# Chunked state-space scan in a decoder trunk: exponentials of the decay sums stored once and loaded per chunk, gate SiLUs in three batches, half products on another schedule

## The chip, the core and the metric

The program runs on one core of one Trainium2 chip. A core has a matrix engine (PE, with weight loads shown apart as PEld), a vector engine (DVE), a scalar engine for activation functions (ACT), a general engine (POOL) and a queue engine (SP) that mainly issues DMAs. Each has its own in-order stream of instructions, and the streams meet only at semaphores. The metric is the device time of one execution in microseconds (us); lower is better.

## What is computed

A trunk of two pre-norm residual layers on 1024 tokens of width 1024. Layer 0 mixes with windowed attention and pooling, layer 1 with a Mamba-2 style scan (SSD); each is followed by a dense SwiGLU. The change is in the scan of layer 1, in this part of the reference:

```python
def ssd_chunked(x, dt, A, Bm, Cm):          # L = 128 tokens, 8 chunks, G = 4 groups of 8 heads
    dA = (dt * A).reshape(b, nc, L, G, hg)
    a_cs = jnp.moveaxis(jnp.cumsum(dA, axis=2), 2, -1)          # the decay sums
    seg = a_cs[..., :, None] - a_cs[..., None, :]
    decay = jnp.exp(jnp.where(causal, seg, -jnp.inf))
    cb = jnp.einsum('bclgn,bcsgn->bcgls', Cc, Bc)
    y_diag = jnp.einsum('bcgls,bcghls,bcsghp->bclghp', cb, decay, xdt)
    ...
    y_off = jnp.einsum('bclgn,bcghpn,bcghl->bclghp', Cc, prev, jnp.exp(a_cs))
    return (y_diag + y_off).reshape(b, s, h, p)
```

Afterwards `y = (scan + x*D) * silu(z)`, where z is one more projection of the input, then a grouped RMS norm and the output projection.

## The kernel before

The matrix products run as three products of split operands (`mm3`: high by high, low by high, high by low, lines L1377 to L1379), so that PE has three 512-column matmuls for each block of 128 inputs. ACT makes the high halves (`hi`, a Copy, L892) and POOL the low ones (`lo`, a subtraction, L721).

The scan stage (`ssd_group`, one function on each engine) runs four times, once for each group of 8 heads: three trips of a loop and a copy behind it. One group is:

- Six projections of 1024 tokens (B, C and four blocks of x) with a short convolution: ACT starts `acc` (L1273), DVE adds three shifted taps (L2448), ACT takes the SiLU (L1282).
- Eight chunks c = 0 to 7 of 128 tokens. For each chunk the row of decay sums comes from DRAM, broadcast over the partitions into `mdec[c % 2]` (L664, a DMA on SP's queue, which for c of 2 and more waits until PE's product of chunk c - 2 has used the buffer). ACT takes `exp` of it into `eacs[c % 2]`, as two activations of 64 partitions (L1301), and then turns `mdec` into the decays in place: eight Relu with a bias per head (L1308) and two Exp over four heads each (L1313). DVE multiplies each half by the masked product of C and B (L2487, `m_ready`). PE has, in this order: the transposes and the C by B product of chunk c + 1 (L1808 to L1813), the states (L1832), the contribution of the carried state (L1837, "yoff"), the diagonal product (L1845, 16 small matmuls, "ydiag"), which waits for both halves of `mdec` and for DVE's `yx` of chunk c - 1, and then some half products of the gate. DVE adds up: token-major copies of chunk c + 1 (`cbm` L2461, `btok` L2464, `xdt` L2468), the state (L2499), `eacs` times yoff (L2506), plus ydiag (L2509), and four `yx` (L2516, `y_ready`). POOL scales `xds` (L846) and `decayed` (L849), and makes the low halves of weights where `LO_AFTER_CHUNK` says.
- The gate z: eight units n (four blocks, two token halves), each made of the half products 2n and 2n + 1, 12 matmuls of 512 columns each. `Z_AFTER_CHUNK` says behind which chunk's ydiag PE does which half products; halves 2 and 3 stand in the code ahead of chunk 0.
- The end: DVE multiplies by the gate (L2476), ACT squares and makes `y_hi` (L1323, L1324), DVE `y_lo` (L2526), and PE starts the output projection (the L1377 rows with `y_hi`), which waits for the `y_lo` of a block before it uses the block. Three outputs are begun with three blocks each before the fourth block is asked for.

The sums themselves are made once ahead of the four groups; DVE copies their transpose to `sumT` and ACT's queue stores it to DRAM (L1257).

Of the kernel before, what the change touches and what calls it, by code (L numbers as in the profile page):

```python
# [27 lines left out]
F32 = mybir.dt.float32  # L28
F32R = mybir.dt.float32r
ALU = mybir.AluOpType  # L30
ACT = mybir.ActivationFunctionType
# [61 lines left out]
def trunk(nc, x, mix_norm_w, ap_w_in, ap_sinks, pool_w, pool_scale, ap_w_out, ssd_w_in, ssd_conv_w,  # L93
# [40 lines left out]
    with ExitStack() as ctx:  # L134
# [79 lines left out]
        gda_lo = at("gda_lo", 4 * S + G * NT * HG, [G * NT * HG], F32R)  # L214
        sumT = at("sumT", 4 * S + 2 * G * NT * HG, [2, P])
        ones = at("ones", 10240 + 3 * NK * SH, [P], F32R)

# [74 lines left out]
        hidden = nc.dram_tensor("hidden", (NP, P, 7 * BANK), F32, kind="Internal").ap()  # L292
        decay_sums = nc.dram_tensor("decay_sums", (G, NT, HG * P), F32, kind="Internal").ap()

        def tail_pair(tt):
# [28 lines left out]
        def down_banks(layer, j):  # L324
# [9 lines left out]
        LO_AFTER_CHUNK = {1: (9,), 2: (10,), 6: (11,), 7: (12, 13)}  # L334
        Z_AFTER_CHUNK = {-1: (0, 1), 0: (4,), 1: (5, 6), 2: (7,), 3: (8, 9), 4: (10, 11), 5: (12,), 6: (13,),
                         7: (14, 15)}
        SILU_AFTER_CHUNK = {1: (0, 1), 3: (2, 3), 5: (4, 5), 7: (6,)}
        GATE_AFTER_CHUNK = {6: (0, 1)}
# [160 lines left out]
        cb_freed, xdt_ready, m_ready = sem("cb_freed"), sem("xdt_ready"), sem("m_ready")  # L499
        relu_done, dec_ready, e_ready = sem("relu_done"), sem("dec_ready"), sem("e_ready")  # L500
        xds_ready, decayed_ready = sem("xds_ready"), sem("decayed_ready")
# [22 lines left out]
        def _(sp):  # L524
# [130 lines left out]
            def ssd_group(g):  # L655
                piece = in_group(g)
                firsts = [g + bc_, g + cc_] + [g * BG + xc + b for b in range(BG)] + [g * BG + zc + b for b in range(BG)]

                def load_decay(c):

                    if c >= 2:
                        sp.wait_ge(ydiag_full, t.count("chunk", c - 1))
                    src = decay_sums[g:g + 1, c, :] if isinstance(g, int) else decay_sums[bass.ds(g, 1), c, :]
                    sp.dma_start(mdec[c % 2][:, :, :].rearrange("p h l -> p (h l)"), src.to_broadcast([P, HG * P]))\  # L664
                        .then_inc(decay_loaded[c % 2], 16)

                for k in range(GP):
                    if k < NCB + BG:
                        load(piece(k), blocks[:, :, bass.ds(firsts[k], 1), :].rearrange("p k j c -> p k (j c)"))
                    else:  # L670
                        b = k - NCB - BG
                        load(piece(k), rows[:, bass.ds(g * BG + b, 1), :].rearrange("p j n -> p (j n)"))
                    if k == 7:
                        sp.wait_ge(sums_stored, 16)
                        load_decay(0)
                    if k == 8:
                        sp.wait_ge(silu_done, t.count("silu", NCB - 1))
                        load_decay(1)
                    for c in DECAY_AFTER_PIECE.get(k, ()):
                        load_decay(c)  # L680
                t.add("chunk", NT)
                t.add("silu", NCB)
# [194 lines left out]
        def _(act):  # L877
# [366 lines left out]
            for k in range(2, LEAD):  # L1244
# [11 lines left out]
            act.wait_ge(sumT_ready, 1)  # L1256
            act.dma_start(decay_sums.rearrange("g c (h l) -> (g c h) l", l=P).rearrange("(a r) l -> r a l", r=P), sumT[:, :, :])\  # L1257
                .then_inc(sums_stored, 16)
            act.wait_ge(dts_v, 5)
            for d, first in ((D[3], GC_DS), (D[7], GC_CD)):  # L1260
                act.activation(gconst[:, :, first:first + NT * HG],
                               d[:, :, :].rearrange("p c s -> p (c s)").rearrange("p (g k) -> p g k", g=G), ACT.Exp)\
                    .then_inc(dts_a, 1)
            t.add("unit")

            def ssd_group(g, last=False):
# [25 lines left out]
                for c in range(NT):  # L1293
                    m = mdec[c % 2]
                    act.wait_ge(decay_loaded[c % 2], t.count("loaded", 16 * (c // 2 + 1)))

                    if c >= 2:
                        act.wait_ge(y_ready, t.count("chunk", c - 1))
                    for odd in range(2):
                        rows = slice(64 * odd, 64 * odd + 64)  # L1300
                        ins = act.activation(eacs[c % 2][rows, :, :], m[rows, odd::2, :], ACT.Exp)  # L1301
                    ins.then_inc(e_ready, 1)
                    act.wait_ge(e_ready, t.count("chunk", c + 1))

# [600 lines left out]
        def _(dve):  # L1906
            t = Tally(unit=0, out=0, tile=0, conv=0, z=0, chunk=0, half=0, carry=0, group=0, rms=0, tail=0,
                      step=0, xhi=0)

# [527 lines left out]
            def ssd_group(g, last=False):  # L2437
# [41 lines left out]
                for c in range(NT):  # L2479
# [20 lines left out]
                    else:  # L2500
                        dve.tensor_copy(state[:, :], ps[:, STATES, :]).then_inc(state_ready, 1)
                    dve.wait_ge(e_ready, t.count("chunk", c + 1))
                    e = eacs[c % 2]
# [15 lines left out]
                t.add("half", 2 * NT)  # L2519
                t.add("carry", NT - 1)  # L2520

                def lo(b, h):
# [46 lines left out]

            dve_loop = dict(unit=NCB, conv=NCB, z=2 * BG, chunk=NT, half=2 * NT, out=2 * NT, carry=NT - 1, group=1, rms=2)  # L2570
            with dve.Fori(0, G - 1) as g:
# [27 lines left out]
```

## Time and profile before

| what | us |
|---|---|
| median of 3 runs | 2396.69 |
| lowest and highest | 2395.57, 2397.83 |
| the profiled execution, own time | 2397.36 |
| its span, first to last instruction | 2395.6 |
| PE busy in it | 2310.4 (96%) |
| POOL, DVE and ACT busy | 1210.8, 1281.2 and 1072.4 |

The span and what lies around it (1.8 us) make the execution's own time. Busy times of different engines overlap. A timeline row gives the start, the duration, the engine and line, the operation, how many instructions are merged in the row, and in brackets how long the engine had been idle before it and what ended that. Durations of neighbours on one engine overlap a little, so a step from start to start is what an instruction costs in a row. A matmul of 512 columns takes 0.23 us from start to start in the stretches where PE's granted clock is 1.0.

### The profile page before, as it was taken

To read this page: it belongs to the slowest core of one execution; us is meant where nothing else is said; L and a number is where in the kernel's file an instruction comes from. 1 tells how busy PE (TensorE), PEld (TensorE's weight loads), DVE (VectorE), ACT (ScalarE), POOL (GpSimd) and SP (SyncE) were. 2 spreads that over 40 slices of the span, in tenths; PEclk is the share of its full clock that TensorE was granted. 3 is DMA by queue.
4 is the path that set the end of the run, shared out by engine and by line. 5 is a ranking of instruction groups with operands and counts; after the bars stand their busy time and mean duration, and the time that the engine had idled before them with its cause. 6 is when DMAs were issued, how large, how long until landed. Compare 5 with 4: busy or idle time off the path is not lost.

```text
span 2395.6 us, 29381 instructions
## 1 busy us (share of the span) xinstructions
PE 2310.4 (96%) x10850; PEld 1880.6 (79%) x10850; DVE 1281.2 (53%) x1660; ACT 1072.4 (45%) x1887; POOL 1210.8 (51%) x852
## 2 busy tenths in 40 slices
PE   6998999999999999999999999999999999999997
PEld 5876778888887788687887887887778888888786
DVE  5446573324334787557348338437772333335776
ACT  4035553333333445457248238239553333333444
POOL 3123278777773554224214314223288778774553
PEclk9999999999999999999999999999999999999999
DMA  5100213223227743221212112122213223227744
GB/s 154 46 27 18 87 63 121 102 108 114 84 97 257 245 150 111 73 63 62 64 43 88 45 53 92 32 71 80 89 62 132 107 91 114 84 97 273 246 149 144
DMA packets 166786, 247.89 MB, mean 103 GB/s; under 512 B 18416, under 2 KB 111484, under 8 KB 164092
## 3 DMA queue, kind: packets, MB, share of 16 engines
q1 hardware_dynamic: 161020, 230.06, 29.1%
q10 hardware_dynamic: 5632, 15.99, 1.7%
q8 instruction: 90, 1.47, 0.3%
q14 instruction: 44, 0.36, 0.0%
HBM read 192.93 MB, written 53.08 MB: 103 GB/s over the span
## 4 chain that ended last, share of the span: by engine, by line
PE 82%; DVE 7%; POOL 3%; ACT 3%; issue 3%; DMA 1%; SPq 0%; DVEq 0%; ACTq 0%; POOLq 0%
PE ps L1377 26%; PE ps L1379 25%; PE ps L1378 25%; POOL p_lo L746 1%; PE ps L1845 1%; POOL p_val L770 1%; DVE acc L2448 1%; PE ps L1400 1%; PE ps L1832 1%; DVE mdec L2487 1%; DMA d_val<-in_w_down 1%; DVE yx L2516 1%; PE ps L1837 1%; PE ps L1563 1%; PE ps L1542 0%
## 5 line engine op out<-in xcount | busy, mean ns | idle before, releaser
L721 POOL TENSOR_TENSOR w_lo<-w_raw,w_hi 128x1024 fp32r<-128x1024 f32 x74 | 182.4, 2468 | 361.0 <-ACT w_hi L892 361.0
L823 POOL TENSOR_TENSOR s_lo<-s_val,s_hi 128x512 fp32r<-128x512 f32 x154 | 231.6, 1507 | 220.4 <-ACT s_hi L1188 220.2
L2119 DVE TENSOR_TENSOR xres<-ps,xres 128x512 f32<-128x512 f32 x132 | 90.7, 688 | 436.6 <-PE ps L1379 425.5
L1377 PE MATMUL ps<-xn_hi,w_hi 128*128 128x512 f32 x800 | 317.9, 397 | 5.6 <-DVE acc L2448 2.6
L1378 PE MATMUL ps<-xn_lo,w_hi 128*128 128x512 f32 x800 | 312.8, 391 | 0.0
L1379 PE MATMUL ps<-xn_hi,w_lo 128*128 128x512 f32 x800 | 312.6, 391 | 0.0
L1377 PE MATMUL ps<-xn_hi,p_hi 128*128 128x512 f32 x704 | 276.3, 392 | 8.9 <-POOL p_lo L746 4.6
L1378 PE MATMUL ps<-xn_lo,p_hi 128*128 128x512 f32 x704 | 275.2, 391 | 0.0
L1379 PE MATMUL ps<-xn_hi,p_lo 128*128 128x512 f32 x704 | 275.1, 391 | 0.0
L746 POOL TENSOR_TENSOR p_lo<-p_val,p_hi 128x512 fp32r<-128x512 f32 x176 | 238.8, 1366 | 43.8 <-ACT p_hi L1007 43.8
L1007 ACT ACTIVATE p_hi<-p_val 128x512 fp32r<-128x512 f32 x176 | 111.1, 632 | 313.4 <-POOL p_val L770 312.4
L1377 PE MATMUL ps<-d_hi,s_hi 128*128 128x512 f32 x616 | 241.5, 392 | 7.4 <-DVE xres L2183 3.4
L1378 PE MATMUL ps<-d_lo,s_hi 128*128 128x512 f32 x616 | 240.4, 390 | 0.0
L1379 PE MATMUL ps<-d_hi,s_lo 128*128 128x512 f32 x616 | 240.2, 390 | 0.0
L1377 PEld LDWEIGHTS ps<-xn_hi,w_hi 128*128 128x128 f32 x800 | 150.8, 189 | 43.1 <-issue 9.8
L2448 DVE SCALAR_TENSOR_TENSOR acc<-ps,gc,acc 128x1023 f32<-128x1023 f32 (+2 forms) x72 | 92.3, 1281 | 172.3 <-ACT acc L1273 170.6
L1188 ACT ACTIVATE s_hi<-s_val 128x512 fp32r<-128x512 f32 x154 | 97.0, 630 | 177.5 <-DMA d_val<-in_w_down 100.7
L1379 PEld LDWEIGHTS ps<-xn_hi,w_lo 128*128 128x128 f32 x800 | 150.9, 189 | 32.1
L1378 PEld LDWEIGHTS ps<-xn_lo,w_hi 128*128 128x128 f32 x800 | 151.1, 189 | 30.1
L892 ACT ACTIVATE w_hi<-w_raw 128x1024 fp32r<-128x1024 f32 x74 | 77.4, 1052 | 208.0 <-PE ps L1379 181.8
L1377 PEld LDWEIGHTS ps<-xn_hi,p_hi 128*128 128x128 f32 x704 | 132.9, 189 | 38.3 <-POOL p_lo L746 6.0
L1379 PEld LDWEIGHTS ps<-xn_hi,p_lo 128*128 128x128 f32 x704 | 133.0, 189 | 27.7
(271 smaller groups left out, 5074.9 us busy)
## 6 DMA issues: line engine op xcount, KB each, us to landing
s_val<-hidden SPq DMA_DIRECT2D x154, 256.0 KB, 2.8
hidden<-xres SPq DMA_DIRECT2D x20, 1792.0 KB, 6.4
wv_g<-in_w_gate SPq DMA_DIRECT2D x22, 1024.0 KB, 5.1
wv_u<-in_w_up SPq DMA_DIRECT2D x22, 1024.0 KB, 5.1
w_raw<-in_ssd_w_in SPq DMA_DIRECT2D x40, 512.0 KB, 3.8
d_val<-in_w_down SPq DMA_DIRECT2D x70, 256.0 KB, 3.8
rows_v<-in_w_down SPq DMA_DIRECT2D x64, 256.0 KB, 3.5
mdec<-decay_sums SPq DMA_DIRECT2D x32, 512.0 KB, 3.7
```

Of the source, the lines that this page charges most:

```text
L721: pool.tensor_tensor(w_lo[piece.slot][:, :], raw[piece.raw][:, :], f(w_hi[piece.slot][:, :]), ALU.subtract).then_inc(lo_done, 1)
L746: pool.tensor_tensor(p_lo[n][:, :, :], src, f(p_hi[n][:, :, :]), ALU.subtract).then_inc(p_lo_done, 1)
L770: pool.tensor_tensor(p_val[n][:, :, :], a, b, op).then_inc(sum_ready, 1)
L823: pool.tensor_tensor(s_lo[i][:, :], s_val[i][:, :], f(s_hi[i][:, :]), ALU.subtract)\
L892: act.activation(w_hi[piece.slot][:, :], raw[piece.raw][:, :], ACT.Copy).then_inc(hi_done, 1)
L1007: act.activation(p_hi[n][:, :, :], src, ACT.Copy).then_inc(p_hi_done, 1)
L1188: act.activation(s_hi[i][:, :], s_val[i][:, :], ACT.Copy).then_inc(s_hi_done, 1)
L1377: pe.matmul(dst, l_hi, r_hi, start=first, stop=False, skip_group_check=reopened)
L1378: pe.matmul(dst, l_hi, r_lo, start=False, stop=False, skip_group_check=reopened)
L1379: return pe.matmul(dst, l_lo, r_hi, start=False, stop=last, skip_group_check=reopened)
L2119: dve.tensor_tensor(tmp, bank, tmp, ALU.add).then_inc(c_ready, 1)
L2448: ins = dve.scalar_tensor_tensor(acc[k % 2][:, shift:], full[:, 0:S - shift], gc[:, tap:tap + 1], acc[k % 2][:, shift:], ALU.mult, ALU.add)
```

## The change

`exp` of the decay sums is taken once, on the transposed sums (`sumE`), ahead of the groups, and stored by ACT's queue to a second DRAM tensor. Per chunk two more DMAs on SP's queue bring it into `eacs`, broadcast over 64 partitions each (`load_e`), behind the load of `mdec` of the same chunk. For c of 2 and more `load_e` waits for `y_ready` of chunk c - 2. ACT loses the two Exp activations per chunk and its wait for `y_ready`; DVE waits for the loads instead of for ACT. The first load of decays waits for both stores. The two tables `Z_AFTER_CHUNK` and `SILU_AFTER_CHUNK` change.

```diff
-        Z_AFTER_CHUNK = {-1: (0, 1), 0: (4,), 1: (5, 6), 2: (7,), 3: (8, 9), 4: (10, 11), 5: (12,), 6: (13,),
-                         7: (14, 15)}
-        SILU_AFTER_CHUNK = {1: (0, 1), 3: (2, 3), 5: (4, 5), 7: (6,)}
+        Z_AFTER_CHUNK = {-1: (0, 1), 0: (4, 5), 1: (6,), 2: (7, 8), 3: (9,), 4: (10, 11), 5: (12,), 6: (13, 14),
+                         7: (15,)}
+        SILU_AFTER_CHUNK = {1: (0, 1, 2), 4: (3, 4, 5), 7: (6,)}
...
+                def load_e(c):
+
+                    if c >= 2:
+                        sp.wait_ge(y_ready, t.count("chunk", c - 1))
+                    src = decay_exps[g:g + 1, c, :] if isinstance(g, int) else decay_exps[bass.ds(g, 1), c, :]
+                    src = src.rearrange("a (b o l) -> a o b l", o=2, l=P)
+                    for odd in range(2):
+                        sp.dma_start(eacs[c % 2][64 * odd:64 * odd + 64, :, :],
+                                     src[:, odd].to_broadcast([64, BG, P])).then_inc(e_loaded[c % 2], 16)
...
-                        sp.wait_ge(sums_stored, 16)
+                        sp.wait_ge(sums_stored, 32)
                         load_decay(0)
                     if k == 8:
                         sp.wait_ge(silu_done, t.count("silu", NCB - 1))
                         load_decay(1)
+                        load_e(0)
+                        load_e(1)
                     for c in DECAY_AFTER_PIECE.get(k, ()):
                         load_decay(c)
+                        load_e(c)
...
+            act.activation(sumE[:, :, :], sumT[:, :, :], ACT.Exp).then_inc(sumE_ready, 1)
+            act.wait_ge(sumE_ready, 1)
+            act.dma_start(sums_of(decay_exps), sumE[:, :, :]).then_inc(sums_stored, 16)
...
-                    if c >= 2:
-                        act.wait_ge(y_ready, t.count("chunk", c - 1))
-                    for odd in range(2):
-                        rows = slice(64 * odd, 64 * odd + 64)
-                        ins = act.activation(eacs[c % 2][rows, :, :], m[rows, odd::2, :], ACT.Exp)
-                    ins.then_inc(e_ready, 1)
-                    act.wait_ge(e_ready, t.count("chunk", c + 1))
...
-                    dve.wait_ge(e_ready, t.count("chunk", c + 1))
+                    dve.wait_ge(e_loaded[c % 2], t.count("loaded", 32 * (c // 2 + 1)))
```

ACT's stream before, from the SiLUs behind chunk 3 to the decays of chunk 6 (chunk 4 and 6 use the first `mdec`, chunk 5 the second; `zs` and `ps` at L1290 are the SiLUs of units 2, 3 and then 4, 5):

```order
L1290 ACTIVATE zs_115<-ps 128x512
L1290 ACTIVATE zs_116<-ps 128x512
L1301 ACT_TABLE_LOAD
L1301 ACTIVATE eacs_100<-mdec_92 64x512 x2
L1308 ACTIVATE mdec_92<-mdec_92,gc 128x128 x8
L1313 ACTIVATE mdec_92<-mdec_92 128x512 x2
L1301 ACTIVATE eacs_101<-mdec_93 64x512 x2
L1308 ACTIVATE mdec_93<-mdec_93,gc 128x128 x8
L1313 ACTIVATE mdec_93<-mdec_93 128x512 x2
L1290 ACT_TABLE_LOAD
L1290 ACTIVATE ps<-ps 128x512 x2
```

The same stretch of the changed kernel, from the decays of chunk 4 (first `mdec`) to those of chunk 5 (second). The SiLUs of units 3, 4 and 5 are at L1310, the Relu at L1319, the Exp at L1324:

```order
L1319 ACTIVATE mdec_93<-mdec_93,gc 128x128 x8
L1324 ACTIVATE mdec_93<-mdec_93 128x512 x2
L1310 ACT_TABLE_LOAD
L1310 ACTIVATE zs_117<-ps 128x512
L1310 ACTIVATE ps<-ps 128x512 x2
L1319 ACTIVATE mdec_94<-mdec_94,gc 128x128 x8
L1324 ACT_TABLE_LOAD
L1324 ACTIVATE mdec_94<-mdec_94 128x512 x2
```

What moved: the SiLU of unit 5 stood behind the decays of chunk 5, and stands ahead of them now. The half products that it waits for, 10 and 11, are behind ydiag of chunk 4 in both kernels.

SP's queue in the changed kernel, last group, from the loads for chunk 2 on (`w_raw` is a piece of the output weights):

```order
L667 DMA mdec_93<-decay_sums 128x1024 [waits ydiag_full]
L677 DMA eacs_101<-decay_exps 64x4x128 [waits y_ready]
L677 DMA eacs_101<-decay_exps 64x4x128
L667 DMA mdec_94<-decay_sums 128x1024 [waits ydiag_full]
L677 DMA eacs_102<-decay_exps 64x4x128 [waits y_ready]
L677 DMA eacs_102<-decay_exps 64x4x128
L543 DMA w_raw<-in_ssd_w_out 128x1024 [waits lo_done] x2
```

What moved: before, the two `mdec` loads and the two weight loads followed each other; now each `mdec` load is followed by two loads of `eacs`, the first of which can hold up what stands behind it.

## Rows read from the trace of the kernel before

**Rows 1.** The page's busy times and its chain, shares of the span by engine.
```profile
PE 2310.4 (96%) x10850; PEld 1880.6 (79%) x10850; DVE 1281.2 (53%) x1660; ACT 1072.4 (45%) x1887; POOL 1210.8 (51%) x852
PE 82%; DVE 7%; POOL 3%; ACT 3%; issue 3%; DMA 1%; SPq 0%; DVEq 0%; ACTq 0%; POOLq 0%
```
**Rows 2.** Waits of PE over the span: total us, times, longest.
```profile
PE ps L1845 <- DVE mdec L2487: 14.5, 13, 2.6
...
PE ps L1377 <- DVE acc L2448: 2.6, 1, 2.6
```
**Rows 3.** PE's timeline, second group: chunks 1, 5, 6, 7.
```profile
1255.92 1.09 PE L1845 MATMUL ps<-mdec,xdt 128*64 128x128 f32 x16 [0.79 <-DVE mdec L2487]
...
1287.43 0.38 PE L1808 MATMUL ps<-CT,BT 128*128 128x128 f32 x2
...
1290.05 1.09 PE L1845 MATMUL ps<-mdec,xdt 128*64 128x128 f32 x16
...
1296.83 1.09 PE L1845 MATMUL ps<-mdec,xdt 128*64 128x128 f32 x16 [0.23 <-DVE mdec L2487]
...
1305.19 1.09 PE L1845 MATMUL ps<-mdec,xdt 128*64 128x128 f32 x16 [2.53 <-DVE mdec L2487]
1306.22 0.50 PE L1377 MATMUL ps<-xn_hi,w_hi 128*128 128x512 f32 x1
...
1311.79 0.39 PE L1377 MATMUL ps<-w_hi,y_hi 128*128 128x512 f32 x1
```
**Rows 4.** ACT's timeline, second group, from chunk 5's decays to chunk 6's.
```profile
1280.51 1.15 ACT L1313 ACTIVATE mdec<-mdec 128x512 f32<-128x512 f32 x2
...
1287.63 0.58 ACT L1290 ACTIVATE ps<-ps 128x512 f32<-128x512 f32 x1 [4.08 <-PE ps L1379]
1288.13 1.05 ACT L892 ACTIVATE w_hi<-w_raw 128x1024 fp32r<-128x1024 f32 x1
1289.19 1.28 ACT L1301 ACT_TABLE_LOAD   x1
1290.49 1.27 ACT L1301 ACTIVATE eacs<-mdec 64x512 f32<-64x512 f32 x2
1291.79 2.45 ACT L1308 ACTIVATE mdec<-mdec,gc 128x128 f32<-128x128 f32 x8
1294.27 1.15 ACT L1313 ACTIVATE mdec<-mdec 128x512 f32<-128x512 f32 x2
```
**Rows 5.** DVE's timeline, second group: chunks 0 and 2, then chunk 6 on.
```profile
1250.70 3.96 DVE L2516 SCALAR_TENSOR_TENSOR yx<-yx,gc,eacs 128x128 f32<-128x128 f32 x4
...
1265.93 0.68 DVE L2506 TENSOR_TENSOR eacs<-ps,eacs 128x512 f32<-128x512 f32 x1
...
1297.70 1.27 DVE L2476 TENSOR_TENSOR yx<-ps,yx 128x512 f32<-128x512 f32 x2
...
1303.86 1.28 DVE L2487 TENSOR_TENSOR mdec<-mdec,cbm 128x512 f32<-128x512 f32 x2
...
1307.13 1.19 DVE L2516 SCALAR_TENSOR_TENSOR yx<-yx,gc,eacs 128x128 f32<-128x128 f32 x4
...
1308.85 3.55 DVE L2526 SCALAR_TENSOR_TENSOR y_lo<-yx,gc,y_hi 128x512 fp32r<-128x512 f32 x3
```
**Rows 6.** Loads of `mdec`: times to landing, from the view of that tile.
```profile
DMA to landing us min/median/max: 3.3/3.7/5.9
```
**Rows 7.** ACT's timeline ahead of the first group.
```profile
993.86 0.73 ACT L1261 ACTIVATE gconst<-dtmp 128x256 f32<-128x256 f32 x2
995.25 1.28 ACT L1273 ACT_TABLE_LOAD   x1 [0.66 <-DVE gc L2440]
```
**Rows 8.** PE's timeline, first group, behind the wait of chunk 7.
```profile
1116.65 0.69 PE L1377 MATMUL ps<-xn_hi,w_hi 128*128 128x512 f32 x1
...
1120.40 0.39 PE L1377 MATMUL ps<-xn_hi,w_hi 128*128 128x512 f32 x1
```
**Rows 9.** The same stretch by windows: PE, PEld, DVE, ACT, POOL busy, granted clock, DMA.
```profile
1118.00:1120.00 2.00, 2.00 (x6) 1.62 (x5) 2.00 (x5) 1.76 (x5) 1.29 (x1) 0.50 0.32 77
```

More of the change, by code:

```diff
@@ L215, in trunk @@
         sumT = at("sumT", 4 * S + 2 * G * NT * HG, [2, P])
+        sumE = at("sumE", 4 * S + 2 * G * NT * HG + 2 * P, [2, P])
         ones = at("ones", 10240 + 3 * NK * SH, [P], F32R)
@@ L293, in trunk @@
         decay_sums = nc.dram_tensor("decay_sums", (G, NT, HG * P), F32, kind="Internal").ap()
+        decay_exps = nc.dram_tensor("decay_exps", (G, NT, HG * P), F32, kind="Internal").ap()
         def tail_pair(tt):
@@ L499, in trunk @@
         cb_freed, xdt_ready, m_ready = sem("cb_freed"), sem("xdt_ready"), sem("m_ready")
-        relu_done, dec_ready, e_ready = sem("relu_done"), sem("dec_ready"), sem("e_ready")
+        relu_done, dec_ready = sem("relu_done"), sem("dec_ready")
+        e_loaded, sumE_ready = [sem("e_loaded0"), sem("e_loaded1")], sem("sumE_ready")
         xds_ready, decayed_ready = sem("xds_ready"), sem("decayed_ready")
@@ L1256, in _, with sums_of @@
             act.wait_ge(sumT_ready, 1)
-            act.dma_start(decay_sums.rearrange("g c (h l) -> (g c h) l", l=P).rearrange("(a r) l -> r a l", r=P), sumT[:, :, :])\
-                .then_inc(sums_stored, 16)
+            def sums_of(dram):
+                return dram.rearrange("g c (h l) -> (g c h) l", l=P).rearrange("(a r) l -> r a l", r=P)
+            act.dma_start(sums_of(decay_sums), sumT[:, :, :]).then_inc(sums_stored, 16)
             act.wait_ge(dts_v, 5)
@@ L1907, in _ @@
             t = Tally(unit=0, out=0, tile=0, conv=0, z=0, chunk=0, half=0, carry=0, group=0, rms=0, tail=0,
-                      step=0, xhi=0)
+                      step=0, xhi=0, loaded=0)
             def step(ins):
@@ L2520, in ssd_group @@
                 t.add("carry", NT - 1)
+                t.add("loaded", 32 * NT // 2)
                 def lo(b, h):
@@ L2568, in ssd_group @@
                 t.add("z", 2 * BG)
-            dve_loop = dict(unit=NCB, conv=NCB, z=2 * BG, chunk=NT, half=2 * NT, out=2 * NT, carry=NT - 1, group=1, rms=2)
+            dve_loop = dict(unit=NCB, conv=NCB, z=2 * BG, chunk=NT, half=2 * NT, out=2 * NT, carry=NT - 1, group=1, rms=2,
+                            loaded=32 * NT // 2)
             with dve.Fori(0, G - 1) as g:
```

## The prediction

> **What bounds the kernel now.** I read the busy times first [rows 1]: PE is busy 96% of the span and holds 82% of the chain that ended last; ACT is busy 45% in all, and at most 3% of the chain is its own. So a change that takes work from ACT pays only where PE waits for ACT, directly or through DVE. The list of PE's waits says how much that can be [rows 2]: all waits for DVE's multiplies of `mdec`, the only ones in the scan's chunks, are 14.5 us. The timeline of the second group shows three that count [rows 3]: 0.79 us at ydiag of chunk 1, 0.23 at chunk 6 and 2.53 at chunk 7, together 3.55 a group, 14.2 in the four groups (the rest of the 14.5 is 0.15 at one chunk 0). The groups repeat each other, so I work out one and multiply by four. The number of matmuls doesn't change. The question is only which waits of PE go and which come.
>
> **Removed: two Exp of 64 partitions per chunk.** They take 1.3 us (1290.49 to 1291.79, [rows 4]), 64 activations in all. ACT also saves one pair of table loads a group, 1.30 us each (1289.19 to 1290.49). None of it stands on PE's path unless ACT is late. At chunk 7 ACT isn't: DVE's own chain is what PE waits for. From the start of ydiag 6 (1296.83) to that of ydiag 7 (1305.19) are 8.36 us [rows 3], and DVE is in work without a gap up to the end of the second multiply of chunk 7 (1303.86 + 1.28 = 1305.14, [rows 5]). The wait of chunk 1 is of the same kind: four `yx` take 3.96 us there, against 1.19 at chunk 7 [rows 5]. What takes these waits away is the new order of half products, not the lighter ACT.
>
> **Moved: half products.** Two of them take 1306.22 to 1311.79, 5.57 us, so one takes 2.79 [rows 3]. Behind chunk 0 there are now two instead of one, ahead of ydiag 1: the 0.79 us is covered, and PE gains it. Behind chunk 6 there are two (13, 14) instead of one, ahead of ydiag 7. PE's own work between ydiag 6 and ydiag 7 was 8.36 - 2.53 = 5.83 and becomes 8.62, against DVE's 8.36: the 2.53 us goes, if DVE's chain stays as long. It may grow, because ACT is early with the last copies of weights and POOL's two subtractions of weights then follow each other beside all four `yx`; at the rate of chunk 0 (3.96 us for the four, [rows 5]) the chain grows by at most 1 us. I take 0.4 us of wait left at chunk 7 (0 to 0.8).
>
> **What that costs at the end.** Half product 14 was cover behind ydiag 7 as well. Before, PE came to the first output product 6.60 us behind the start of ydiag 7 (1311.79 - 1305.19, [rows 3]). Now, with one half product left, it comes at 6.60 - 2.79 = 3.81. It needs the three `y_lo`, which end at 1310.03, 1311.22 and 1312.40 (1308.85 plus thirds of 3.55, [rows 5]), that is 4.84, 6.03 and 7.21 us behind ydiag 7. This chain starts with ydiag 7 itself, so it can't come earlier. Three matmuls of one block take 0.68. Without waits the third block would start at 3.81 + 1.36 = 5.17; it starts at 7.21. PE waits 2.0 us (1.8 to 2.2) in three pieces.
>
> **Moved: SiLU of unit 5.** This is the term that decides. It waits for half product 11, on PE behind ydiag 4. Before, the same wait stood behind the decays of chunk 5: those were ready at 1281.66, then ACT idled 4.08 us for PE [rows 4], and nobody missed it, since PE had the decays of chunk 5 and needed those of chunk 6 only at 1296.6. In the changed order ACT stands at this SiLU with the decays of chunk 5 not begun. Queued behind it, by rows 3 and 4, from the end of half product 11 (1287.43): 0.20 to the SiLU's start, 0.50 for it, 2.48 for the eight Relu (1291.79 to 1294.27), 1.30 table load, 1.15 for the two Exp, some 0.06 to DVE, 0.68 for DVE's second multiply (half of 1.28, plus the overlap), 0.05 to PE: 6.42 us. PE has the products of chunk 6's tokens, the states and yoff in that time, 1290.05 - 1287.43 = 2.62 us. ydiag 5 waits 3.80 us (3.6 to 4.0), where it waited for nothing before. Having more lead elsewhere doesn't help, since the chain begins with PE's own half product.
>
> A rule bears on the 1.30. The Trainium skill (ScalarE: Activation LUTs, What ACT_TABLE_LOAD costs) gives 2.66 us for every switch, load and drain. By it ydiag 5 would wait 1.36 us longer, 5.4 us more in four groups. The row goes against it: the next activation starts 1.30 behind the load's start. The sum goes by the row.
>
> **Behind the late ydiag 5** DVE does what it does between ydiag 6 and 7, less the two gate multiplies (1.20 of the row of 1.27): 8.36 - 1.20 = 7.16 us to ydiag 6. PE's own work there is 1296.83 - 0.23 - 1290.05 = 6.55 us [rows 3]. ydiag 6 waits 0.6 us (0.4 to 1.0).
>
> **Added: DMAs.** Two loads a chunk, 64 in all, of 128 KB each into SBUF. The trace has none like them. From below they cost nothing, since SP has time and DVE needs `eacs` late: for chunk 2 the load may go when `yx` of chunk 0 ends (1254.66), and DVE multiplies at 1265.93 [rows 5], 11.3 us later, against 3.7 us for a load of four times the size and 5.9 at the worst [rows 6]. From above, a load as late as twice the worst would make DVE wait some 0.5 us a chunk, which PE mostly has no slack for: 24 chunks by 0.5 are 12 us. I take 0, the value of the nearest row. What is queued behind `load_e` on SP (the next `mdec` load) waits for ydiag one chunk earlier, which itself waits for the `y_ready` in question. The weight loads move by about a chunk and are used chunks later. The single Exp and its store lie ahead of the first group: ACT ends the two Exp at 994.59 and its next load starts at 995.25 [rows 7]; 0.4 for the Exp (a half of 0.73 and its end) and some 0.5 for the store's issue make it 0.3 late, at a place where PE waits 2.6 us for this chain [rows 2]. Cost 0.3 us (0 to 0.6).
>
> **The clock.** In the first group the 2.53 us wait of chunk 7 was followed by slow matmuls: nine of them from 1116.65 to 1120.40, 3.75 us instead of 9 by 0.23 [rows 8], at a granted clock of 0.50, the 1.2 GHz level [rows 9]. That is 1.7 us. In the second group the same wait was followed by full speed (24 matmuls in 5.57 us, [rows 3]). The trace so has it both ways. The new wait of 3.8 us is longer; I take two falls in four groups. Each costs 1.7, of which the 0.6 us wait of chunk 6 takes up its part, so 1.1; the fall of the first group, at chunk 7, goes with its wait. 2 x 1.1 - 1.7 = 0.5 us (-1.7 with none, +2.7 with four; +5 if the waits behind take up nothing).
>
> By the Trainium skill (TensorE: Matmul & The Clock Gate, HAM oscillation) an idle PE is put back to the low clock and pays for it after each gap. By that rule all four waits of chunk 5 fall, and the time is 2 us above my sum. The trace agrees only in part, with the one fall above.
>
> **The sum.** New waits per group: 3.8 + 0.6 + 0.4 + 2.0 = 6.8. Old ones that go: 3.55. Net 3.25 a group, 13.0 in four. With 0.3 and 0.5: 13.8 us on the profiled execution's 2397.36, 2411.2. That execution is 0.67 above the median of the runs, which gives 2410.5. Bounds: from below 3.6 + 0.4 + 0 + 1.8 - 3.55 = 2.25 a group, 9.0, less 1.7 for the clock: 2404. From above 4.0 + 1.0 + 0.8 + 2.2 - 3.55 = 4.45, 17.8, with 0.6 and 5: 2420.
>
> **Rivals.** First, the change does what its parts suggest: the waits of 14.2 us go and nothing comes, 2382.5. For it speaks that each of the three waits does get cover. Against it the order of ACT's stream: the SiLU of unit 5 can't start before half product 11 has ended, and PE has 2.6 us of work for a chain of 6.4. It decides if the decays of chunk 5 can be ready by other means; I see none. 6%. Second, no change that can be measured: only the wait at chunk 5 comes, 3.80 against 3.55 that go, 0.25 a group, and 2398. It needs the `y_lo` to be in time for one half product, where the rows say 2 us late, and POOL not to slow DVE's `yx` behind ydiag 5 (1.19 instead of about 3). 8%. Third, slower for another reason as well: the loads of `eacs`, in pieces of 512 bytes, land late, and DVE waits in most chunks. With the bound above, 12 us on top: 2422. It decides from about 11 us between `y_ready` and the end of the load. 6%. Fourth, the clock falls behind each wait of chunk 5 and nothing absorbs it: 2415, inside my range and part of the forecast.
>
> **Chances.** Forecast with its clock cases, 2404 to 2420: 77%. First rival 6%, second 8%, third 6%, anything slower still 3%. The range 2402 to 2422 takes in the bounds and the third rival's price, and leaves out about 2 in 10. A measurement of this kernel tells some 0.2% (4.8 us) from no change. Faster by more than that 0.07, within it 0.09, slower 0.84.
>
> **What would show it.** In the changed kernel's trace: at ydiag of chunk 5, in each group, PE idle for about 3.8 us and released by DVE's multiply, DVE idle before it and released by ACT's Exp, ACT idle before the third SiLU of the batch and released by PE. No wait at chunk 1. At chunk 7 under 1 us. Ahead of the first output products three short waits for `y_lo`, 2 us in all. PE's waits for `mdec` over the span about 19 us instead of 14.5, and about 8 for `y_lo`. No wait of DVE for a DMA into `eacs`. I would be wrong if ydiag 5 starts at once, or if DVE waits for the loads.

## The result and the profile after

| kernel | median us | lowest, highest | ratio to before, 95% interval |
|---|---|---|---|
| before, beside it | 2397.02 | 2395.57, 2397.83 | |
| changed | 2420.73 | 2413.97, 2426.17 | 1.0098 [1.0072, 1.0125] |

The changed kernel is slower by 23.7 us of median; the forecast was +13.8. Its profiled execution took 2419.34 us with a span of 2417.6, so 22.0 us more span than before. The page has these two lines in place of [rows 1]: busy times, then the chain that ended last.

```profile
PE 2320.9 (96%) x10850; PEld 1885.8 (78%) x10850; DVE 1273.6 (53%) x1660; ACT 1021.5 (42%) x1816; POOL 1209.3 (50%) x852
...
PE 83%; DVE 7%; POOL 3%; issue 3%; ACT 2%; DMA 1%; ACTq 0%; DVEq 0%; SPq 0%; POOLq 0%
```

ACT has 50.9 us less work, as the diff says, and it is worth nothing. PE has the same 10850 matmuls and was busy 10.5 us longer with them, and it idled 11.5 us longer (2417.6 - 2320.9 = 96.7 us, against 2395.6 - 2310.4 = 85.2). These two make the 22.0.

PE's waits over the span, against [rows 2] (total us, times, longest):

```profile
PE ps L1856 <- DVE mdec L2498: 18.7, 10, 3.8
...
PE ps L1388 <- DVE y_lo L2538: 8.3, 8, 1.8
...
PE ps L1388 <- DVE acc L2459: 2.9, 1, 2.9
```

The waits for the decays went from 14.5 to 18.7 us, the waits for `y_lo` are new with 8.3, and the one ahead of the first group grew by 0.3. That is 12.8 us; other waits took 1.3 off. PE's timeline of the second group, against [rows 3] (start, duration, engine, line, and in brackets the idle time before it and what ended that), shows the diagonal products of chunks 5, 6 and 7, then the first output products:

```profile
1289.09 0.38 PE L1819 MATMUL ps<-CT,BT 128*128 128x128 f32 x2
...
1295.53 1.98 PE L1856 MATMUL ps<-mdec,xdt 128*64 128x128 f32 x16 [3.76 <-DVE mdec L2498]
1297.44 0.79 PE L1388 MATMUL ps<-xn_hi,w_hi 128*128 128x512 f32 x1
...
1304.59 1.09 PE L1856 MATMUL ps<-mdec,xdt 128*64 128x128 f32 x16
...
1314.34 1.09 PE L1856 MATMUL ps<-mdec,xdt 128*64 128x128 f32 x16 [1.23 <-DVE mdec L2498]
...
1319.31 0.47 PE L1388 MATMUL ps<-w_hi,y_hi 128*128 128x512 f32 x1 [0.93 <-DVE y_lo L2538]
...
1321.00 0.47 PE L1388 MATMUL ps<-w_hi,y_hi 128*128 128x512 f32 x1 [0.75 <-DVE y_lo L2538]
```

The chain behind the 3.76 stands on ACT's timeline, against [rows 4]. In order: SiLU of unit 5, eight Relu of chunk 5, table load, two Exp.

```profile
1289.29 0.58 ACT L1310 ACTIVATE ps<-ps 128x512 f32<-128x512 f32 x1 [8.04 <-PE ps L1390]
1289.78 2.43 ACT L1319 ACTIVATE mdec<-mdec,gc 128x128 f32<-128x128 f32 x8
1292.23 1.28 ACT L1324 ACT_TABLE_LOAD   x1
1293.53 1.15 ACT L1324 ACTIVATE mdec<-mdec 128x512 f32<-128x512 f32 x2
```

DVE's timeline continues it: it had nothing to do for 8.32 us, then multiplied, and PE started when the second multiply had ended.

```profile
1294.19 1.29 DVE L2498 TENSOR_TENSOR mdec<-mdec,cbm 128x512 f32<-128x512 f32 x2 [8.32 <-ACT mdec L1324]
```

ACT, with least work of all, idled 8.04 us and then was late. From the start of PE's products of chunk 6's tokens, just behind half product 11 (1289.09), to ydiag 5 (1295.53) are 6.44 us; the prediction's chain said 6.42.

The 10.5 us more of PE's busy time is the clock. The windows behind ydiag 5 of the same group (columns: PE, PEld, DVE, ACT, POOL busy, granted clock, DMA share, GB/s) show it at 0.50, its 1.2 GHz level:

```profile
1295.50:1297.50 2.00, 1.97 (x17) 1.64 (x17) 2.00 (x5) 2.00 (x8) 0.94 (x1) 0.50 0.00 0
1297.50:1299.50 2.00, 2.00 (x6) 1.61 (x6) 1.93 (x4) 1.97 (x5) 2.00 (x3) 0.50 0.37 137
```

In the two microseconds of the second window PE began four matmuls of 512 columns, 0.43 us apart (the x6 counts those that reach into it too), where full speed, 0.23 us apart, has nearly nine. The 16 small matmuls of ydiag 5 took 1.98 us in the timeline above, 1.09 at full speed.

### The profile page after: what moved, and what is told of

The parts are those of the page before. It is cut to its first block, busy times and chain, and to the rows that moved or that the text cites. A ratio compares the mean times of both kernels' runs of the same rounds, so it can differ in the third digit from the quotient of the medians.

```text
span 2417.6 us, 29435 instructions
## 1 busy us (share of the span) xinstructions
PE 2320.9 (96%) x10850; PEld 1885.8 (78%) x10850; DVE 1273.6 (53%) x1660; ACT 1021.5 (42%) x1816; POOL 1209.3 (50%) x852
## 4 chain that ended last, share of the span: by engine, by line
PE 83%; DVE 7%; POOL 3%; issue 3%; ACT 2%; DMA 1%; ACTq 0%; DVEq 0%; SPq 0%; POOLq 0%
PE ps L1388 26%; PE ps L1389 26%; PE ps L1390 26%; POOL p_lo L762 1%; PE ps L1856 1%; POOL p_val L786 1%; DVE yx L2527 1%; PE ps L1411 1%; PE ps L1843 1%; DMA d_val<-in_w_down 1%; PE ps L1574 1%; DVE y_lo L2538 0%; PE ps L1553 0%; PE ps L1848 0%; PE ps L1824 0%
## 5 line engine op out<-in xcount | busy, mean ns | idle before, releaser
L862 POOL TENSOR_TENSOR xds<-xdt,gc 128x512 f32<-128x512 f32 x32 | 33.5, 1047 | 252.7 <-DVE xdt L2479 252.7
```

The source lines that it names most:

```text
L862: pool.tensor_tensor(heads(xds), heads(xdt[c % 2]), factor(GC_DS), ALU.mult).then_inc(xds_ready, 1)
```

## The experiments

My theory after the result: the order of the two tables makes the loss, by the SiLU of unit 5 first of all; the loads and the saved exponentials are worth nothing; the part that the forecast lacks is the clock behind the new waits. The rivals: the loads cost or gain by themselves, and the move of half product 14 is what costs. All times in one table first. Kernels of a batch share a chip and the runs of before: the first four have 2395.91 us, the next four 2397.5, the last two 2397.97.

| label | median us | ratio to before, interval | PE waits for `mdec`, `y_lo` (us) | PE busy (us) |
|---|---|---|---|---|
| silu5_back | 2397.26 | 1.0009 [0.9999, 1.0018] | 5.9, 8.3 | 2312.0 |
| loads_alone | 2408.73 | 1.0057 [1.0043, 1.0071] | 23.0, none | 2314.8 |
| tables_alone | 2427.71 | 1.0125 [1.0107, 1.0143] | 27.1, 6.7 | 2320.4 |
| gap_filled | 2415.76 | 1.0080 [1.0066, 1.0094] | 14.6, 4.3 | 2325.5 |
| loads_lo12 | 2398.31 | 0.9999 [0.9990, 1.0008] | 14.3, none | 2312.6 |
| half14_back | 2425.70 | 1.0118 [1.0102, 1.0134] | 30.2, none | 2320.8 |
| new_tables | 2380.70 | 0.9933 [0.9919, 0.9947] | 1.8, none | 2309.5 |
| three_last | 2386.73 | 0.9952 [0.9939, 0.9966] | 1.7, 4.4 | 2310.3 |
| new_tables_exps_on_act | 2383.61 | 0.9946 [0.9931, 0.9960] | 2.0, 2.3 | 2309.8 |
| new_tables_again | 2381.47 | 0.9940 [0.9927, 0.9952] | 1.8, none | 2309.6 |

### One SiLU put back

```diff
-        SILU_AFTER_CHUNK = {1: (0, 1, 2), 4: (3, 4, 5), 7: (6,)}
+        SILU_AFTER_CHUNK = {1: (0, 1, 2), 4: (3, 4), 5: (5,), 7: (6,)}
```

> The changed kernel with one SiLU moved back: unit 5 behind the decays of chunk 5 instead of ahead of them; the half products and the loads of the exponentials stay. Theory (ACT's order makes PE wait): ydiag of chunk 5 starts at once, the 3.76 us wait and the low clock behind it go in all four groups; left are about 0.2 us at chunk 6, 1 to 1.5 at chunk 7 and 1.8 ahead of the outputs, in sum near the 3.55 of the kernel before. Time 2393 to 2398, and little spread. Rival (the loads of the exponentials on SP cost the time): still some 15 us above the kernel before, 2410 or more.

Measured 2397.26 us, some 23 below the changed kernel and level with before. The low spread that I expected did not come: eleven runs lie between 2393.88 and 2402.96. PE's waits:

```profile
PE ps L1388 <- DVE y_lo L2538: 8.3, 8, 1.8
...
PE ps L1856 <- DVE mdec L2498: 5.9, 10, 2.0
```

The four waits of 3.76 us are gone, and PE's busy time falls from 2320.9 to 2312.0. So one place in ACT's stream holds practically the whole loss: 12.8 us less waiting for `mdec` and 8.9 us less of slow matmuls. It also shows that the rest of the change is a wash: 8.6 us of waits for `mdec` are gone, 8.3 for `y_lo` have come.

### The loads alone, the tables alone

loads_alone is the changed kernel with both tables as before; tables_alone is the kernel before with both tables of the changed one, the exponentials still on ACT. The first has this edit, the second its reverse on the kernel before:

```diff
-        Z_AFTER_CHUNK = {-1: (0, 1), 0: (4, 5), 1: (6,), 2: (7, 8), 3: (9,), 4: (10, 11), 5: (12,), 6: (13, 14),
-                         7: (15,)}
-        SILU_AFTER_CHUNK = {1: (0, 1, 2), 4: (3, 4, 5), 7: (6,)}
+        Z_AFTER_CHUNK = {-1: (0, 1), 0: (4,), 1: (5, 6), 2: (7,), 3: (8, 9), 4: (10, 11), 5: (12,), 6: (13,),
+                         7: (14, 15)}
+        SILU_AFTER_CHUNK = {1: (0, 1), 3: (2, 3), 5: (4, 5), 7: (6,)}
```

> The changed kernel with both tables as before the change: only the exponentials are taken once and loaded. Theory: the same three waits of PE as before (about 0.9 at chunk 1, 0.2 at 6, 2.5 to 3.5 at 7), so 2396 to 2400, no gain from the lighter ACT. Rival (the loads cost): 2405 or more, with DVE or ACT waiting for DMAs in the profile where PE then waits.

> The kernel before with the two new tables: the exponentials stay on ACT in every chunk. Theory: the chain behind half product 11 is longer by the two Exp of 64 partitions, 1.3 us, so ydiag of chunk 5 waits about 5.0 us in each group instead of 3.76, and the time is at or above that of the changed kernel, 2418 to 2430. Rival (the loads cost the time): near the kernel before, 2400 or less.

tables_alone took 2427.71 us, 7 above the changed kernel (the intervals of the two ratios overlap), with waits at ydiag 5 of 5.20 us. Its exponentials stand in the chain behind the SiLU, and the rows of ACT's timeline show the 1.27 us in their place:

```profile
1290.14 0.58 ACT L1290 ACTIVATE ps<-ps 128x512 f32<-128x512 f32 x1 [8.62 <-PE ps L1379]
1290.74 1.28 ACT L1301 ACT_TABLE_LOAD   x1
1292.03 1.27 ACT L1301 ACTIVATE eacs<-mdec 64x512 f32<-64x512 f32 x2
1293.34 2.45 ACT L1308 ACTIVATE mdec<-mdec,gc 128x128 f32<-128x128 f32 x8
```

loads_alone was a miss: I expected no change, and it is 13 us slower than before. PE waits 4.66 us at chunk 7 where it waited 2.53 [rows 3]. In order: POOL's (GpSimd's) subtractions for weight pieces 12 and 13, DVE's four `yx` of chunk 6, and PE's diagonal product of chunk 7.

```profile
1299.17 2.35 POOL L737 TENSOR_TENSOR w_lo<-w_raw,w_hi 128x1024 fp32r<-128x1024 f32 x1
1301.96 2.43 POOL L737 TENSOR_TENSOR w_lo<-w_raw,w_hi 128x1024 fp32r<-128x1024 f32 x1 [0.44 <-ACT w_hi L908]
1299.44 5.10 DVE L2527 SCALAR_TENSOR_TENSOR yx<-yx,gc,eacs 128x128 f32<-128x128 f32 x4
1305.80 1.98 PE L1856 MATMUL ps<-mdec,xdt 128*64 128x128 f32 x16 [4.66 <-DVE mdec L2498]
```

DVE's four `yx` end just behind the second subtraction (1304.54 and 1304.39). They take 1.14 us where POOL is idle, 3.0 to 4.0 beside one whole subtraction, 5.10 beside two. Before, ACT had exponentials to take and handed over the copy of piece 13 later: there the four end at 1303.93 and the second subtraction starts at 1304.13. Counted from the start of ydiag 6, the second subtraction starts at 7.30 us before and at 6.61 in loads_alone, and in both the fourth `yx` comes up at some 6.77. ACT, relieved, set off POOL sooner, and 0.7 us was enough for POOL to stand in DVE's way. The time lies in the range of the rival (the loads cost), but its sign is missing: no instruction of DVE waits for a load of `eacs`, and ACT's one wait for a DMA here, 0.82 us for piece 13 at 1300.82, makes POOL's second subtraction later and not earlier.

### The subtraction moved

```diff
-        LO_AFTER_CHUNK = {1: (9,), 2: (10,), 6: (11,), 7: (12, 13)}
+        LO_AFTER_CHUNK = {1: (9,), 2: (10,), 6: (11, 12), 7: (13,)}
```

This is loads_alone with that line.

> The kernel of loads_alone (exponentials loaded, half products and SiLUs where before has them) with one number moved: GpSimd takes the low half of weight piece 12 behind chunk 6 and no longer behind chunk 7. In loads_alone the diagonal products of chunk 7 waited 4.65 us in each group where before waits 2.53, and the trace has GpSimd's subtractions of pieces 12 and 13 back to back (1299.17 and 1301.96) beside VectorE's y of chunk 6, which took 5.10 us instead of 3.01. Theory (ScalarE, without its exponentials, hands over piece 13 some 2 us sooner, the two subtractions join up and VectorE's y lasts longer): with piece 12 out of the way y of chunk 6 takes 1.2 to 2.2 us, the wait at chunk 7 falls to 0.5 to 1.5 us in each group, the time falls by 14 to 20 us to 2388 to 2395. Rival (the wait comes from the decay sums or from the loads of the exponentials, which SyncE issues between other transfers): wait and time stay, 4.2 to 4.8 us and 2406 to 2412.

The wait at chunk 7 went altogether in the first and second group (0.70 us is left in the third and fourth), and the time fell by 10.4 us to 2398.31 (by 12.0 if each kernel is set against the runs of before beside it), less than the 14 to 20 expected. It only comes back to the level of before. The rows say why. The pair of subtractions now stands one chunk earlier, and does there what it did at chunk 7:

```profile
1289.24 2.41 POOL L737 TENSOR_TENSOR w_lo<-w_raw,w_hi 128x1024 fp32r<-128x1024 f32 x1
1292.00 2.36 POOL L737 TENSOR_TENSOR w_lo<-w_raw,w_hi 128x1024 fp32r<-128x1024 f32 x1 [0.35 <-ACT w_hi L908]
...
1289.28 5.49 DVE L2527 SCALAR_TENSOR_TENSOR yx<-yx,gc,eacs 128x128 f32<-128x128 f32 x4
1300.12 1.14 DVE L2527 SCALAR_TENSOR_TENSOR yx<-yx,gc,eacs 128x128 f32<-128x128 f32 x4
...
1296.03 1.98 PE L1856 MATMUL ps<-mdec,xdt 128*64 128x128 f32 x16 [2.42 <-DVE mdec L2498]
```

`yx` of chunk 5 takes 5.49 us instead of 3.30, `yx` of chunk 6 takes 1.14 instead of 5.10, and PE waits 2.42 us at chunk 6 instead of 4.66 at chunk 7. The rival, late loads or late decay sums, would have left wait and time where they were: it falls. The expectation had piece 13 handed over 2 us sooner; counted from ydiag 6 it was the 0.7 us above.

### The gap filled with dummy matmuls

14 matmuls of 512 columns, into the bank that ydiag overwrites anyway, run ahead of ydiag of chunk 5 in the changed kernel; their sums are thrown away.

```diff
+                    if c == 5:
+                        pe.wait_ge(y_ready, t.count("chunk", c))
+                        for k in range(14):
+                            pe.matmul(ps[:, YDIAG, :], xn_hi[:, k % NK, 0:P], xn_hi[:, k % NK, 0:BANK], start=True, stop=True)
```

> The changed kernel with 14 more matmuls of 512 columns on PE ahead of ydiag of chunk 5, into the bank that ydiag then overwrites; they add no result and take about 3.2 of the 3.76 us in which PE stood idle. Theory (the part of the loss above the waits is the clock, which falls behind the wait): the clock stays high at chunk 5, the end of each group comes 1 to 2 us earlier, 2409 to 2416, and the spread of the runs shrinks. If the clock has no part in it, the time stays at 2420 or rises by the 0 to 2 us that the added work may cost.

Measured 2415.76 us, 5.0 below the changed kernel, with 56 matmuls more. ydiag 5 still starts when its chain ends, but at full speed:

```profile
1294.10 1.09 PE L1860 MATMUL ps<-mdec,xdt 128*64 128x128 f32 x16 [0.56 <-DVE mdec L2502]
...
1301.53 1.09 PE L1860 MATMUL ps<-mdec,xdt 128*64 128x128 f32 x16 [0.86 <-DVE mdec L2502]
```

So the clock behind ydiag 5 depends on the wait ahead of it. What the falls cost in time can't be read from the difference of the two kernels, though: 5.0 us by the medians, where the intervals of the two ratios overlap, and 4.3 by the profiled spans. Of the 4.3, 1.8 us arise ahead of the first group, where the changed kernel's profiled execution had a fall behind the setup wait and this one had none. From the start of ydiag 5 to that of ydiag 6 the changed kernel takes 8.07, 9.06, 8.04 and 7.97 us in the four groups and this one 7.42 or 7.43: a fall costs 0.5 to 1.6 us there, 0.9 on average. Behind that most of it comes back. ydiag 7 waits 2.0 us in every group of gap_filled, and 0, 1.23, 0 and 1.51 in the changed kernel. From ydiag 5 to the start of the next group's first diagonal product the changed kernel takes 148.09, 151.04 and 147.58 us, this one 148.41, 148.48 and 148.48. So of these three groups only the second ends sooner, by 2.6 us, and there the changed kernel also has the fall behind `y_lo`; the expected 1 to 2 us for each group did not come. In busy time a fall costs more, about 1.8 us by the start-to-start times of the changed kernel's matmuls, and the next waits take up the difference: the changed kernel has no wait at chunk 6, and this one has 0.84 to 0.86. The runs spread over 7.5 us here.

### Half product 14 put back

```diff
-        Z_AFTER_CHUNK = {-1: (0, 1), 0: (4, 5), 1: (6,), 2: (7, 8), 3: (9,), 4: (10, 11), 5: (12,), 6: (13, 14),
-                         7: (15,)}
+        Z_AFTER_CHUNK = {-1: (0, 1), 0: (4, 5), 1: (6,), 2: (7, 8), 3: (9,), 4: (10, 11), 5: (12,), 6: (13,),
+                         7: (14, 15)}
```

> The changed kernel with half product 14 back behind chunk 7, as before has it. Theory of the prediction: half 14 (2.73 us) hid part of the wait at chunk 7 and left 2 us uncovered ahead of the first output products, so it was nearly a wash: the diagonal products of chunk 7 now wait 3.4 to 4.2 us in each group, the waits for the low part of y (about 2 us) go, time 2418 to 2428. Rival (the move of half 14 is what costs the 9 us that the prediction lacks): 2405 to 2414.

Measured 2425.70 us. The 8.3 us of waits for `y_lo` went, and ydiag 7 waited 2.15, 4.01, 4.11 and 3.91 us in the four groups, 14.2 instead of 2.74; the first is below the 3.4 to 4.2 expected. The move was no cause of the loss; it was worth some 5 us, though the intervals of the two ratios overlap.

### Two new tables

```diff
+        Z_AFTER_CHUNK = {-1: (0, 1), 0: (4, 5), 1: (6,), 2: (7,), 3: (8, 9), 4: (10,), 5: (11,), 6: (12, 13),
+                         7: (14, 15)}
+        SILU_AFTER_CHUNK = {1: (0, 1, 2), 4: (3, 4), 6: (5,), 7: (6,)}
```

three_last has these instead, and the moved subtraction of loads_lo12:

```diff
+        Z_AFTER_CHUNK = {-1: (0, 1), 0: (4, 5), 1: (6,), 2: (7,), 3: (8,), 4: (9,), 5: (10, 11), 6: (12,),
+                         7: (13, 14, 15)}
+        SILU_AFTER_CHUNK = {1: (0, 1, 2), 5: (3, 4), 6: (5,), 7: (6,)}
+        LO_AFTER_CHUNK = {1: (9,), 2: (10,), 6: (11, 12), 7: (13,)}
```

> The changed kernel with tables drawn from the waits found: half products behind chunks 0 to 7 as 4 5 / 6 / 7 / 8 9 / 10 / 11 / 12 13 / 14 15, SiLUs 0 1 2 behind chunk 1, 3 4 behind chunk 4, 5 behind chunk 6, 6 behind chunk 7. If the waits are those of the prediction's chain (no SiLU between a half product that ends late and decays that are due), no diagonal product waits over 0.3 us, about 1.5 us for the low part of y stay: 2.2 us for each group below before, 2384 to 2391. If GpSimd's subtractions of pieces 12 and 13 still stand beside y of chunk 6, chunk 7 waits 1 to 2 us more: 2392 to 2398.

> The changed kernel with half products 4 5 / 6 / 7 / 8 / 9 / 10 11 / 12 / 13 14 15 behind chunks 0 to 7, SiLUs 0 1 2 behind chunk 1, 3 4 behind chunk 5, 5 behind chunk 6, 6 behind chunk 7, and the low half of weight piece 12 on GpSimd behind chunk 6. If both causes are found (the SiLU ahead of due decays, GpSimd's two subtractions beside y of chunk 6), only chunk 7 still waits, 0.4 to 1.2 us, and the three halves cover the low parts of y: 2.6 to 3.3 us for each group below before, 2381 to 2387. If piece 12 isn't a cause, chunk 7 waits 2 to 3 us and the time is 2388 to 2394.

new_tables takes 2380.70 us, 0.7% below before and 40 us below the changed kernel, and 2381.47 when run again. That is 3 us better than the 2384 to 2391 expected. PE's waits for the diagonal products:

```profile
PE ps L1856 <- DVE mdec L2498: 1.8, 8, 0.2
```

No wait for `y_lo` is listed, and a window over 60 us of the second group's scan has PE busy for 59.55 of them at a granted clock of 1.00:

```profile
1240.00:1300.00 60.00, 59.55 (x383) 47.40 (x382) 52.61 (x94) 44.20 (x93) 27.60 (x21) 1.00 0.39 123
```

three_last, which I had put below new_tables, is 6 us above it. It removes the waits at chunk 7 as well (one of 0.74 us at chunk 4 of the last group is new), but piece 13 is late there: POOL's subtraction (at 1298.93, 2.40 us) now lies beside the start of DVE's `y_lo`, with POOL's squares (`sq`) close behind it; three `y_lo` take 5.25 us there, 3.09 in new_tables, and PE waits 4.4 us for them in all. These waits are 4.4 of the 6 us.

### Is it the loads that allow the new order?

new_tables_exps_on_act is the kernel before with the two tables of new_tables and nothing else.

> The kernel before with the tables of new_tables: the exponentials of the decay sums stay on ScalarE, nothing is stored for them or loaded. ScalarE has 1.27 us more to do for each chunk, in the stretches where it waits for half products or decay sums anyway. Theory (order alone sets the time, the loads carry none of the gain): no diagonal product waits over 0.5 us in the loops, 2379 to 2386. Rival (the loads make the room that the new order needs): the diagonal products of chunks 1, 3 or 7 wait 1 us or more, 2388 to 2397.

> new_tables once more, beside the run with the exponentials on ScalarE, on one chip: 2379 to 2384 as before. Theory: within 4 us of that run. Rival (the loads make the room): 6 to 15 us below it.

2383.61 us (2380.26 to 2388.90) against 2381.47 (2380.11 to 2386.24); the intervals of the two ratios overlap. PE's waits differ by 2.3 us for `y_lo`:

```profile
PE ps L1377 <- DVE y_lo L2526: 2.3, 4, 0.6
PE ps L1845 <- DVE mdec L2487: 2.0, 9, 0.2
```

Two tables, without a single added DMA, have all but perhaps 2 us of the gain.

## Why the prediction was right, and where its size was off

**The direction and the mechanism.** Slower, by the SiLU of unit 5 standing ahead of the decays of chunk 5: in the trace as forecast, and silu5_back shows it by undoing it.

| step of the prediction | forecast | measured |
|---|---|---|
| new wait at ydiag 5, a group | 3.80 | 3.76, 3.76, 3.77, 3.76 |
| wait of chunk 1 goes | 0.79 | gone in all groups |
| wait at ydiag 6, a group | 0.6 | none |
| wait at ydiag 7, a group | 0.4 (0 to 0.8) | 0, 1.23, 0, 1.51 |
| waits for `y_lo`, a group | 2.0 | 2.49, 1.68, 2.49, 1.67 |
| setup | 0.3 | 0.3 |
| loads of `eacs` | 0 | 0 |
| PE's waits for `mdec`, span | about 19 | 18.7 |
| PE's waits for `y_lo`, span | about 8 | 8.3 |
| clock | +0.5 (busy +1.7, waits taken up -1.2) | busy +10.5 |

Waits come out at 12.8 us in the three lines of the wait list, against 13.3 forecast (13.0 and 0.3 for the setup). That they agree so well is partly luck: ydiag 6 was forecast 2.4 too high over the four groups and ydiag 7 1.1 too low (2.74 against 1.6), and 0.23 at chunk 2 in each group was not forecast at all. The 0.6 at ydiag 6 was no bad reading: where the clock stays high, in gap_filled, that wait is 0.84 to 0.86, and in the changed kernel the slow matmuls took it up. The `y_lo` waits came in two pieces a group, not three.

**The mis-sized term is the clock.** The step that failed is "I take two falls in four groups". The clock fell behind ydiag 5 in all four groups, and also twice elsewhere: behind the setup wait of 2.87 us (13 matmuls at 0.41 to 0.43 us instead of 0.23, and a first one at 0.59: 2.8 us) and behind the `y_lo` waits of the second group (seven at 0.43, some 1.6 us). The price of one fall was near: 1.7 us of busy time forecast, about 1.8 measured, and 0.9 on average up to ydiag 6 (by gap_filled) against the 1.1 of the forecast. The number of falls was not. Four of 1.8, 2.8 at the setup and 1.6 at `y_lo`, less the 1.7 that go, are 9.9 of the 10.5. The Trainium skill's section named in the prediction (TensorE: Matmul & The Clock Gate, HAM oscillation), by which every such gap is paid for, was right for the gaps of chunk 5, and I gave it too little weight because the trace of before had one fall behind four waits of 2.53. The wait was longer than that, 3.76 us.

Over all the kernels run here, each of the 19 waits of 3.76 us or more ahead of a diagonal product (changed kernel 4, half14_back 7, loads_alone 4, tables_alone 4) was followed by matmuls at the 1.2 GHz level. Of those from 2.0 to 2.6 us ahead of a diagonal product some were and some weren't: one of four in before, two of four in loads_lo12, two of four in gap_filled, none of two in silu5_back, and the one of 2.15 us in half14_back was. The setup wait of 2.87 us was followed by the low level in four of the nine profiled executions that have it (changed kernel, silu5_back, loads_lo12, new_tables_again). Part of the +10.5 is therefore chance of the profiled execution. The four runs of the changed kernel spread over 12 us (2413.97 to 2426.17), but silu5_back, without the falls of chunk 5, spreads over 9 in eleven runs, so the spread isn't shown to be these falls.

**ydiag 7.** The prediction named the coupling (ACT early, POOL's two subtractions beside all four `yx`) but priced it by the row of chunk 0, 3.96 us. Where the two do stand beside the four `yx`, in the second and the fourth group, these take 5.24 and 5.17 us. The second group:

```profile
1307.57 2.40 POOL L737 TENSOR_TENSOR w_lo<-w_raw,w_hi 128x1024 fp32r<-128x1024 f32 x1
1310.31 2.37 POOL L737 TENSOR_TENSOR w_lo<-w_raw,w_hi 128x1024 fp32r<-128x1024 f32 x1 [0.34 <-ACT w_hi L908]
1307.84 5.24 DVE L2527 SCALAR_TENSOR_TENSOR yx<-yx,gc,eacs 128x128 f32<-128x128 f32 x4
```

In the first group piece 13 comes late from DRAM (ACT waits 0.98 us for it at 1116.41), the subtraction starts after the four, they take 3.06 us, and nothing waits at chunk 7; the third group is alike. The 0.4 of the forecast stands against 0.69 on average, made of two groups with none and two with 1.23 and 1.51, so that it came near was luck. The fault mattered more where I used it for an experiment: loads_alone was expected at no change.

**The rivals.** The intended gain (2382.5) didn't come with this order, but new_tables gets just that, 2380.7, by another: the prediction saw no other means to have the decays of chunk 5 ready, and was wrong there, since half product 11 one chunk later and its SiLU behind chunk 6 are such means. The break-even rival fell with the `y_lo` waits and the clock. Late loads fell: the landing times of `eacs` are these (min, median, max), and no instruction of DVE waits for them.

```profile
DMA to landing us min/median/max: 2.8/3.1/5.3
```

**What stays open.** How much of the time, and not only of PE's busy time, the falls cost over a whole group: gap_filled moves the wait at chunk 7 as well. The last 1.7 us between the profiled difference (22.0) and that of the medians (23.7) are inside the spread of the runs. Why the clock fell behind some waits near 2.5 us and not behind others of the same length wasn't settled.

## To carry to other kernels

Work taken off an engine that isn't the bound gains nothing by itself, and it moves whatever that engine sets off: here a lighter ACT alone cost 13 us through POOL and DVE. In an in-order stream put an instruction that waits for the bound engine's newest product behind all work that is already due, never ahead of it; then count what PE has to do between giving that product and needing the result. And when a wait on PE becomes longer than those behind which the trace shows full speed, price the clock as falling behind every one of them, as it did here behind 19 of 19; then ask how much of it the next waits take up.

## What the chip showed that I had not expected

DVE's `yx` (one instruction, a 128x128 tile with two operands in SBUF) takes 1.14 us for four alone, and beside POOL's subtraction doesn't run at a lower rate but stops until POOL's instruction is over. The view of these four instructions in loads_alone (min, median, max in ns) shows it:

```profile
L2527 DVE SCALAR_TENSOR_TENSOR yx<-yx,gc,eacs x4: 340/1283/2423, 1299.4 to 1302.1; 128x128 f32<-128x128 f32 x4
```

The longest lasts as long as one whole subtraction (2.43 us), the shortest is undisturbed, and the subtractions took their usual 2.35 and 2.43. It goes the other way too: in silu5_back a subtraction that began 0.04 us behind the start of DVE's two multiplies of `mdec` (1302.24, 1.28 us for the two) took 3.50 us. The Trainium skill (SBUF — State Buffer, Who interferes with whom) says that a DVE instruction with two inputs in SBUF and a GpSimd instruction that reads SBUF exclude each other, and that the one that starts first holds the port for its whole length. The traces agree with both halves. So the price of a meeting is the rest of the other's instruction: long subtractions beside short `yx` are the costly pairing, and a second subtraction that begins before the fourth `yx` does holds that one up as well.
